# Output projection with x turned between its tiles, memory keys normed beside the sample rows, score rows between decay steps, early memory tiles

## What is computed

```python
def memory_kv(mem, lp):
    hm = rms_norm(mem, lp['norm_mem'])
    k = rms_norm((hm @ lp['w_ck']).reshape(B, M, H_C, DH_C), lp['ck_norm'])
    v = (hm @ lp['w_cv']).reshape(B, M, H_C, DH_C)
...
def finish_layer(x, y_m, y_a, mem_k, mem_v, conv_hist, lp):
    x = x + jnp.concatenate([y_m, y_a.astype(y_m.dtype)], axis=-1) @ lp['w_out']
    h = rms_norm(x, lp['norm_cross'])
    q = rms_norm((h @ lp['w_cq']).reshape(B, T, H_C, DH_C), lp['cq_norm'])
    ... softmax over the memory keys, w_co, then a gated ConvFFN (w_up, w_down)
...
        h_m, (c_p, n_p, m_p) = mlstm_prompt(...)          # 4 mLSTM heads over 512 rows
        y_a = dsa_prompt(...)                             # 4 sparse softmax heads
        mk_p, mv_p = memory_kv(mem_prompt, lp)
        xp, conv_p = finish_layer(xp, y_m, y_a, mk_p, mv_p, ...)
        h_s, (c_s, n_s, m_s) = mlstm_sample(...)          # one row and one 128x128 state per head, 8 times
        y_as = dsa_sample(...)                            # 256 keys and values gathered from a paged cache
```

## Time and profile before

| | |
|---|---|
| median of 3 runs | 1365.85 us (1362.71 to 1368.11) |
| profiled execution, its time | 1363.25 us |
| its span in the trace | 1361.5 us |
| PE busy, matmuls / weight loads | 1139.3 us (84%) / 1000.9 us |
| DVE busy | 587.4 us (43%) |
| ACT busy | 486.0 us (36%) |
| POOL busy | 401.0 us (29%) |
| granted clock, mean of the span | 0.90 |

### The profile page before, as it was taken

One profiled execution on the slowest core, in us unless ns is written; L12 is line 12 of the kernel. 1 busy time (PEld: TensorE's weight loads), 2 busy tenths in 40 slices (PEclk: granted clock), 3 DMA queues, 4 the chain that ended last, 5 costly groups with the idle time before them and its releaser, 6 DMA issues.

```text
span 1361.5 us, 20030 instructions
## 1 busy us (share of the span) xinstructions
PE 1139.3 (84%) x7911; PEld 1000.9 (74%) x7911; DVE 587.4 (43%) x1105; ACT 486.0 (36%) x870; POOL 401.0 (29%) x200
## 2 busy tenths in 40 slices
PE   4788967657884586797687999988999999999998
PEld 4788857657873242686677986652999999998997
DVE  3405486886566566454513124552333334430000
ACT  5222242333244254123013454231355555543212
POOL 2212211122120112275121314540244444443442
PEclk9977788789897687799798999997899999999999
DMA  5223211113220112465161211844133332223222
GB/s 141 63 51 78 63 32 31 47 57 84 68 73 0 49 48 82 139 196 178 31 232 47 63 47 34 311 166 139 47 92 93 92 92 88 87 86 91 85 85 90
DMA packets 165331, 121.82 MB, mean 89 GB/s; under 512 B 7383, under 2 KB 154421, under 8 KB 164974
## 3 DMA queue, kind: packets, MB, share of 16 engines
q1 hardware_dynamic: 149536, 96.35, 23.6%
q10 hardware_dynamic: 12848, 14.08, 3.1%
q0 software_dynamic: 2880, 10.49, 2.7%
HBM read 111.81 MB, written 9.27 MB: 89 GB/s over the span
## 4 chain that ended last, share of the span: by engine, by line
PE 68%; DVE 15%; ACT 6%; issue 6%; DMA 2%; POOL 1%; ACTq 1%; DVEq 0%; POOLq 0%; SPq 0%
PE PS L237 43%; PE PS L912 3%; PE PS L1879 3%; PE PS L387 2%; DMA raw<-in_w_out 1%; PE PS L1368 1%; PE PS L2332 1%; ACT ikc L470 1%; PE PS L1839 1%; PE PS L1825 1%; DVE rw L314 1%; DVE tk L581 1%; PE PS L1112 1%; PE PS L953 1%; DVE tiny L580 1%
## 5 line engine op out<-in xcount | busy, mean ns | idle before, releaser
L237 PE MATMUL PS<-ahi,whi 128*128 128x260 f32 (+1 forms) x1456 | 311.9, 297 | 26.5 <-POOL wlo L2720 9.9
L1626 POOL TENSOR_TENSOR wlo<-raw,whi 128x1024 fp32r<-128x1024 f32 x84 | 201.0, 2393 | 415.9 <-ACT whi L831 415.9
L237 PE MATMUL PS<-alo,whi 128*128 128x260 f32 (+1 forms) x1456 | 302.1, 290 | 0.0
L237 PE MATMUL PS<-ahi,wlo 128*128 128x260 f32 (+1 forms) x1456 | 301.5, 290 | 0.0
L237 PEld LDWEIGHTS PS<-ahi,whi 128*128 128x128 f32 (+1 forms) x1456 | 235.1, 197 | 31.8 <-issue 18.1
L237 PEld LDWEIGHTS PS<-alo,whi 128*128 128x128 f32 (+1 forms) x1456 | 233.8, 196 | 0.0
L237 PEld LDWEIGHTS PS<-ahi,wlo 128*128 128x128 f32 (+1 forms) x1456 | 233.0, 195 | 0.0
L831 ACT CAST whi<-raw 128x1024 fp32r<-128x1024 f32 x108 | 113.1, 1048 | 317.0 <-PE PS L237 295.1
L2720 POOL TENSOR_TENSOR wlo<-raw,whi 128x1024 fp32r<-128x1024 f32 (+1 forms) x31 | 73.2, 2361 | 293.0 <-ACT whi L2758 293.0
L2459 DVE SCALAR_TENSOR_TENSOR PS<-ub,cw,PS 128x512 f32<-128x512 f32 x44 | 33.2, 755 | 156.0 <-ACT PS L2437 156.0
L237 PE MATMUL PS<-gHi,whi 128*128 128x260 f32 x352 | 71.1, 283 | 0.0
(11 more groups left out here) (502 smaller groups left out, 1870.7 us busy)
## 6 DMA issues: line engine op xcount, KB each, us to landing
raw<-in_w_up SPq DMA_DIRECT2D x44, 512.0 KB, 3.8
raw<-in_w_in SPq DMA_DIRECT2D x30, 512.0 KB, 3.8
ckv<-in_cache_mem_v SPq DMA_DIRECT2D x8, 1024.0 KB, 5.4
raw<-in_w_down SPq DMA_DIRECT2D x16, 448.0 KB, 3.8
raw<-in_w_ck SPq DMA_DIRECT2D x8, 512.0 KB, 4.5
raw<-in_w_cv SPq DMA_DIRECT2D x8, 512.0 KB, 4.3
raw<-in_w_out SPq DMA_DIRECT2D x8, 512.0 KB, 4.1
ckv<-in_cache_mem_k ACTq DMA_DIRECT2D x4, 1024.0 KB, 10.6
```

The costliest lines, as they stand in the source:

```text
L237: ins = nc.tensor.matmul(out[0:m, half, 0:HALF], w[:, s, k, 0:m], x[:, k0 + k, half * HALF:(half + 1) * HALF], start=(first and k == 0 and ...
L1626: nc.gpsimd.tensor_tensor(wlo[:, s], raw[:, s], whi[:, s].bitcast(F32), ALU.subtract).then_inc(split_full[s], 1)
```

## The change

- **Heads.** The sample row's key product gets banks of its own (`PJ[1]`) and its own semaphore `k_row`. PE issues it ahead of step 0 (even rows) or behind the next head's gate rows (odd rows); DVE multiplies ahead of decay step 2 and sums behind step 3.
- **Softmax and loop.** Memory tiles 0, 1 and 2 go between the softmax's steps; the loop's iterations take the tiles that `ROW_TILES` lists: 3, then two each, then 14 and 15 alone. The scores get a region of their own, `sp_row`. POOL's order of weights and gathers follows. SP's order stays as it was.
- **Keys' norm.** ACT squares the finished keys in iterations 4 and 5, ahead of the state store, and DVE multiplies them behind iteration 6. The four passes behind the loop go.
- **Behind the loop.** `vec_split_y` of the mLSTM heads comes behind the sample rows' last steps; PE starts the first output tile on the attention inputs (k = 4 to 7), which are split long before, then takes k = 0 to 3 as they come. x is turned in two batches, behind output tiles 0 and 1. Sums of squares, key turning and key copies lie between the output tiles. `act_cache` waits for the residual of output tile 1 of pair 1.
- **Query.** The norm writes all eight blocks into `hs8` and then splits; PE takes the first two query tiles together, high parts first, low parts behind.

The diff, without semaphore lists and regions:

```diff
-            for b in range(B):
-                for t in (2 * b + 2, 2 * b + 3):
+            for t in (2, 3, 4):
+                pool_weights(pool, t)
+            for b in range(2, B):
+                pool.wait_ge(v_used, b - 1)
+                gather("cache_v", b)
+                for t in (2 * b + 1, 2 * b + 2):
                     pool_weights(pool, t)
...
+            pool_weights(pool, 17)
...
         def pe_satt_k(pe, b):
...
+            if b < 2:
+                pe.wait_ge(hm_lo, 4)
+            else:
+                pe.wait_ge(k_used, 2 * (b - 1))
+            nc.tensor.matmul(PJ[1][:, b % 2, :], rowsel[:, b, :], sw[:], start=True, stop=True).then_inc(k_row, 1)
...
+            dve.wait_ge(k_row, b + 1)
+            V(v.tensor_tensor(kprod[:], skv[:, b % 2], PJ[1][:, b % 2, :].unsqueeze(1).to_broadcast([P, 2, MIX]), ALU.mult))
             dve.sem_inc(k_used, 2)
+
+        def vec_satt_sum(dve, b):
...
             pe_ml_score(pe, h, 1)
+            pe_satt_k(pe, 2 * h)
             pe_ml_nd(pe, h, 0)
...
             pe_ml_nd(pe, h, 2)
-            pe_satt_k(pe, 2 * h)
             pe_ml_nd(pe, h, 3)
...
-            vec_satt_k(dve, 2 * h)
+                    vec_satt_k(dve, 2 * h)
+            vec_satt_sum(dve, 2 * h)
...
+        ROW_TILES = [(3,), (4, 5), (6, 7), (8, 9), (10, 11), (12, 13), (14,), (15,)]
...
-                pe_mem_step(pe, 2 * b)
+                pe_mem_step(pe, ROW_TILES[b][0])
                 pe_satt_v(pe, b)
-                pe_mem_step(pe, 2 * b + 1)
-            pe_mem_back(pe, 15)
+                for t in ROW_TILES[b][1:]:
+                    pe_mem_step(pe, t)
             pe.wait_ge(sst_ready, 1)
...
-            for h in range(H):
-                vec_split_y(dve, alo[:, h, 0:SEQ], z_m[:, 3 * H + h, 0:SEQ], ahi[:, h, 0:SEQ], H + h + 1)
+                if b == 6:
+                    vec_key_norm(dve)
...
+                if b in (4, 5):
+                    act_key_squares(act, b - 4)
                 act.wait_ge(sc_in, b + 1)
...
+        def act_key_squares(act, mt):
+
+            for s in range(2):
+                act.wait_ge(out_free[s], mem_base(6 + s) + 1)
+            for h in range(H):
+                S(nc.scalar.activation(md[:, 0:2 * DH], mk_t[:, mt, h * 2 * DH:(h + 1) * 2 * DH], ACT.Square,
+                                       accum_out=xc[:, mt * H + h:mt * H + h + 1]))
...
+            pe.wait_ge(k_used, 2 * B)
+            pe_mem_step(pe, 0)
             pe_satt_soft(pe)
+            pe_mem_step(pe, 1)
+            pe_satt_turn(pe)
+            pe_mem_step(pe, 2)
             pe_mls(pe)
...
+            for h in range(H):
+                vec_split_y(dve, alo[:, h, 0:SEQ], z_m[:, 3 * H + h, 0:SEQ], ahi[:, h, 0:SEQ], H + h + 1)
...
+        def pe_out_first(pe):
+
+            pe.wait_ge(split_full[0], BASE["out"][0] + 1)
+            pe.wait_ge(out_free[0], BASE["out"][0])
+            for half in range(2):
+                for n, k in enumerate((4, 5, 6, 7, 0, 1, 2, 3)):
+                    pe.wait_ge(y_lo, Y_PARTS if half else H if k >= H else H + k + 1)
...
         def pe_out_proj(pe):
 
+            pe_out_first(pe)
+            pe_turn_in(pe, 0, 4)
+            pe_out_tile(pe, 0, 1)
+            pe_turn_in(pe, 4, KT)
+            for i in range(1, 4):
+                pe_out_tile(pe, i, 0)
+                for f in (2 * i - 2, 2 * i - 1):
+                    pe_sumsq(pe, 1, f, sq2, T)
+                if i == 3:
+                    pe_mem_keys(pe, 0, 4)
+                pe_out_tile(pe, i, 1)
+            pe_sumsq(pe, 1, 6, sq2, T)
+            pe_mem_keys(pe, 4, 6)
+            pe_sumsq(pe, 1, 7, sq2, T)
+            pe_mem_keys(pe, 6, KT)
...
+            for k in range(KT):
+                v.scalar_tensor_tensor(hs8[:, k], xT[:, k], gains[:, G_CROSS + k:G_CROSS + k + 1], rstd2[:], ALU.mult,
+                                       ALU.mult).then_inc(hs_ready, 1)
+            for k in range(KT):
+                dve.wait_ge(nhi_ready, KT + k + 1)
+                v.tensor_tensor(alo[:, k], hs8[:, k], ahi[:, k].bitcast(F32), ALU.subtract).then_inc(nlo_ready, 1)
...
-            stage_done(dve, "ck", out_free)
...
-            V(v.tensor_tensor(q4, k4, k4, ALU.mult))
-            V(v.tensor_reduce(xc[:, 0:8], q4, AX, ALU.add), ck_ss)
-            dve.wait_ge(ck_rstd, 1)
-            V(v.tensor_tensor(k4, k4, xc[:, 0:8].unsqueeze(2).to_broadcast([P, 8, 2 * DH]), ALU.mult))
-            V(v.tensor_tensor(k4, k4, ckg[:].unsqueeze(1).to_broadcast([P, 8, 2 * DH]), ALU.mult), mk_ready)
...
+            for k in range(KT):
+                pe.wait_ge(nhi_ready, KT + k + 1)
+                for s in range(2):
+                    for w in (whi, wlo):
+                        for half in range(2):
+                            nc.tensor.matmul(PJ[s][:, half, 0:HALF], w[:, s, k, :], ahi[:, k, half * HALF:(half + 1) * HALF],
+                                             start=(k == 0 and w is whi), stop=False)
...
-            act.wait_ge(out_free[0], BASE["out"][0] + 1)
+            act.wait_ge(out_free[1], BASE["out"][1] + 1)
```

More of the change, by code:

```diff
@@ L1632, in act_squares @@
             nc.scalar.activation(sq2[:, f % 2], xT[:, f], ACT.Square).then_inc(sq_ready, 1)
-        def pe_out_proj(pe):
+        def pe_out_first(pe):
[4 more added lines that the diff above has]
+                    pe.wait_ge(y_lo, Y_PARTS if half else H if k >= H else H + k + 1)
+                    for j, (w, x) in enumerate(((whi, ahi), (whi, alo), (wlo, ahi))):
+                        m = nc.tensor.matmul(PJ[0][:, half, 0:HALF], w[:, 0, k, :], x[:, k, half * HALF:(half + 1) * HALF],
+                                             start=(n == 0 and j == 0), stop=(n == KT - 1 and j == 2))
+            m.then_inc(w_used[0], 1)
@@ L1700, in act_norm, with pe_turn_in @@
                 nc.scalar.copy(hi[:, k, 0:width], hs2[:, k % 2, 0:width]).then_inc(nhi_ready, 1)
-        def pe_turn_in(pe):
+        def pe_turn_in(pe, k0, k1):
             pe.wait_ge(x_in_s, 16 * (NTT + 1) + 16 * 6)
-            for k in range(KT):
-                bank = pe_bank(pe, 2 + k % 2)
+            if k0 == 0:
+                bank = pe_bank(pe, 2)
+                for k in range(KT):
+                    m = nc.tensor.transpose(bank[:, k * B:(k + 1) * B], xs_re[:, k * P:(k + 1) * P], ident[0:B, 0:B])
+                m.then_inc(bank_full[2], 1)
+            for k in range(k0, k1):
+                bank = pe_bank(pe, 3 - k % 2)
@@ L1737, in vec_mem_keys @@
+        def vec_mem_keys(dve, f0, f1):
+            v = nc.vector
+            for f in range(f0, f1):
                 V(v.tensor_scalar(mkT[:, f], rd_bank(dve, 2 + f % 2)[:, 0:NMEM], gains[:, G_CQ + f % 2:G_CQ + f % 2 + 1], SCALE_C,
@@ L1739, in vec_mem_keys, with pe_mem_keys @@
                 dve.sem_inc(kn_ready, 1)
[L1741 to L1746 removed]
+        def pe_mem_keys(pe, f0, f1):
             pe.wait_ge(mk_ready, 1)
[L1748 removed]
+            for f in range(f0, f1):
                 bank = pe_bank(pe, 2 + f % 2)
@@ L1887, in pe_co, with pe_query_first @@
             m.then_inc(w_used[s], 1)
+        def pe_query_first(pe):
+            for s in range(2):
+                pe.wait_ge(split_full[s], BASE["cq"][s] + 1)
+                pe.wait_ge(out_free[s], BASE["cq"][s])
+            for k in range(KT):
+                pe.wait_ge(nhi_ready, KT + k + 1)
+                for s in range(2):
+                    for w in (whi, wlo):
+                        for half in range(2):
+                            nc.tensor.matmul(PJ[s][:, half, 0:HALF], w[:, s, k, :], ahi[:, k, half * HALF:(half + 1) * HALF],
+                                             start=(k == 0 and w is whi), stop=False)
+            for k in range(KT):
+                pe.wait_ge(nlo_ready, KT + k + 1)
+                for s in range(2):
+                    for half in range(2):
+                        m = nc.tensor.matmul(PJ[s][:, half, 0:HALF], whi[:, s, k, :], alo[:, k, half * HALF:(half + 1) * HALF],
+                                             start=False, stop=(k == KT - 1))
+                    if k == KT - 1:
+                        m.then_inc(w_used[s], 1)
         def pe_fused(pe):
             base = BASE["cq"]
-            for n in range(KT):
+            pe_query_first(pe)
+            pe.wait_ge(kn_ready, KT)
+            pe.wait_ge(bank_read[1], filled[1])
+            for n in range(2):
+                pe_slot(pe, n)
+            for n in range(2, KT):
                 s = n % 2
```

152 lines of the change are left out of this document (72 added, 80 removed).

## The result

The changed kernel takes 1346.9 us (median of 4 runs, 1346.17 to 1348.92) where the kernel before has 1365.95 (1362.71 to 1368.11): a ratio of 0.9865, 95% interval 0.9842 to 0.9887. It is faster by 19 us, half of the 37 that were forecast, and the time lies 4 us above the range of the forecast (1312 to 1343). The profiled execution took 1348.92 us, span 1347.2, 14.3 shorter than the span before.

The account below looks back on a forecast made before the run. Only 457 to 756 us mattered: DVE and ACT's chain bounds the heads, PE the loop, waits and half clock much behind it. Gains 9.0 + 3.6 + 24.5 = 37.1 us gave 1329 us, range 1312 to 1343.

Parts of the forecast that it names:

- Heads, 9.0: Four heads: moving key row and product shortens the chain, 1.4 us in head 0 and 2.5 in each other; 9.0 us.
- The product fits the gap: Heads: DVE's key product (1.22 us) fits DVE's 1.26 us wait ahead of decay step 2, so 2.66 leave the chain.
- the heads don't shorten: Heads: ACT's exponentials wait for later decay sums, most of 19.3 us a head stays; +7, 1336 us; chance 0.10.
- Softmax, 0: Stretch between heads and loop: three early memory tiles fill PE's idle time and lose nothing; 0 us taken.
- Loop, 3.6: Memory loop: three tiles fewer save 13.9 us, waits give 10 back, 0.3 for the softmax; gain 3.6 us.
- The ring: Loop: state store, next state load, weight tile, cast and next store wait in a circle; 10.4 us a turn against PE's 10.02.
- 5, 13 and 15: Loop: memory tiles ahead of which PE would wait for ACT's copies; waits put at 2.3, 3.8 and 2.4 us.
- The 13.9 us: Loop: PE's own work falls from 84.4 to 70.5 us when three tiles leave, before any waits.
- The rival that it doesn't close (1318): Loop: stores or weights land faster and SP keeps ahead; the loop gains 13.9 us, time 1318; chance 0.15.
- Behind the loop, 24.5: From the loop to the third query tile: reordered output, turning, norm and query work takes 93.5 us, not 118.0; gain 24.5.
- the wait for the last weight tile: Output tiles: cache loads still delay the last weights, holding ACT; PE idles 3.3 us, then two sums at half clock, 3.8.
- The clock at the turns, a rival of 0.18: Output tiles: the clock falls while x is transposed, five tiles each take 2.4 us longer; +12, 1341 us; chance 0.18.

Follow-up runs that it names:

- the runs with and without the part: Only the heads' edits put into the kernel before: 0.9944, 1357.2 us; only those edits taken out of the changed kernel: 0.9898, 1348.6 us.
- the ten profiles: Profiles with the changed kernel's head code: heads of 73.4 us four times, 78.3 twice, 81.6 four times; old head code took 80.3 and 80.4.
- the matmuls that fed PE: Changed kernel plus matmuls whose result nobody reads, 16 at the wait for a head's squares, 8 behind the early key row: 0.9819, 1340.3 us.

## Why the prediction was wrong

**Heads, 9.0: the step that failed in the trace, by 7 us, and on average by less.** "The product fits the gap" held, and a head whose decay steps ran at full clock took what was named (16.5 in one profile, 16.8 forecast). The sum took every duration at the clock of one execution: it counted the key row at 1.1 to 1.44, on a stretch that had a clock of 0.84, and did not ask where half clock would fall once the order changed. The row took 2.07 and step 0 2.05 to 2.08 where it fell on them. On average the miss is 1 to 5 us by the runs with and without the part, 6 by the ten profiles. The rival that the heads don't shorten was there, with another cause and too small a chance.

**Softmax, 0: the step that failed outright, -4.9.** I weighed half clock on the first tile (3.5) and took none, and I never priced POOL: the three early tiles bring two subtractions into DVE's chain. The trace of before had the row. In the loop, where DVE has slack, the state multiply stood at 1.74 us seven times beside POOL, as here:

```profile
570.05 1.74 DVE L1421 TENSOR_TENSOR cb<-cb,Qb 128x512 f32<-128x512 f32 x1
...
568.84 2.39 POOL L845 TENSOR_TENSOR wlo<-raw,whi 128x1024 fp32r<-128x1024 f32 x1 [2.66 <-ACT whi L831]
```

Its neighbours of the same shape take 0.69. The Trainium skill states the rule (page "SBUF — State Buffer", section "Who interferes with whom": a DVE instruction with two SBUF inputs contends with a GpSimd instruction that reads SBUF, and the port pair that they share is an exclusive lock). By it the gate step would have been priced at up to a whole subtraction, 2.4 us; the trace agrees, with 2.17 us for it and 2.07 for the sum of sample outputs (2.26 in place of 0.19).

**Loop, 3.6: the mechanism was right, the size 2.5 off.** The ring closes, at tiles 7 and 13 (2.33 and 2.42 us, where I named 5, 13 and 15). The waits themselves came to 4.75 us and not the 9.0 that were taken; what was missing is half clock: some 1.5 us behind each of the two waits, 1.4 in tile 15, and above all the loop's start. That the two errors nearly cancel is luck. The 13.9 us set iterations at full clock against the 84.4 measured, and 84.4 holds 4.2 us more than eight iterations of 10.02, since the loop began at half clock. It still does, before and after:

```profile
553.16 3.78 PE L1368 MATMUL PS<-s_tok,rowsel 8*128 8x512 f32 x4 [1.68 <-DVE Qb L1411]
```

```profile
557.45 3.78 PE L1382 MATMUL PS<-s_tok,rowsel 8*128 8x512 f32 x4 [1.68 <-DVE Qb L1426]
```

These row products take 1.91 at full clock; with the tile behind them in the changed kernel, 3.0 us of the 13.9 never went. The keys' multiplies, 6.1 us, cost nothing in this stretch: PE waits for them behind it, 1.59 us. The rival that it doesn't close (1318) has the wrong sign.

**Behind the loop, 24.5: 19.9.** Named and found: the wait for the last weight tile (3.85 and sums at half clock), that ahead of the third query tile (3.58, and 1.7 of half clock behind it), no wait for DVE's residual. Missed: the first output tile, done 13.7 us in and not 9.0, since it starts behind those 1.59 us, at half clock, and DVE, ahead of the splits, stands 2.1 us behind POOL.

**The clock at the turns, a rival of 0.18**: it did not fall there. The second batch of transposes lies in this row of the changed kernel:

```profile
660.00:670.00 10.00, 9.58 (x81) 9.11 (x79) 3.46 (x5) 2.22 (x3) 2.38 (x1) 1.00 0.29 86
```

The rule of the Trainium skill that was weighed there (page "TensorE: Matmul & The Clock Gate", section "Part 4: PE-mode transpose") finds no support in this kernel: the tiles behind both batches, of under 3 us each, ran at full clock. The rival's time, 1341, was nearest to the result all the same, by luck: the four terms above made the miss, and its mechanism none of it.

**The range** had room for one failed term. In the trace four failed with one sign: 7.1, 4.9, 2.5 and 4.6 us, 19 in all.

## What to carry to other kernels

Before work is moved beside a chain on DVE, list what POOL will run in that time and look in the trace for DVE instructions that are longer than others of their shape. Where the clock falls to half at waits, price each step that is moved at both levels, and take several profiles of the same code before a stage's length is believed. An order of loads that waits for a store is tested first by putting one load ahead of it: that was worth 9 us here. Edits that each help alone can meet on one engine: test them together.

## What the runs showed that was not expected

The heads' length comes in three values with the same instructions, 73.4, 78.3 and 81.6 us, and the time of a run goes, by and large, with its mean clock: the changed kernel on one chip took 1339.7 us at 0.904 and 1345.6 at 0.896 (though also 1348.3 at 0.900), the kernel before on another 1358.3 at 0.903 and 1368.3 at 0.894. What sets the moment at which the clock falls stays open: the matmuls that fed PE went with a clock of 1.00 in the last two heads only, and no run moved that moment alone.

A DVE instruction on 8x4 elements took 2.32 us in place of 0.15 beside POOL's subtraction of 128x1024, while a reduction and a multiply with one input in PSUM beside such subtractions, in the loop, kept their 0.69 us.
